# Seven block products for nine tenths of the last gate and up projections, with weight sums made by adding DMAs and VectorE

## The chip, the cores and the metric

The kernel runs on one NeuronCore of a Trainium2 chip. The metric is the time of one execution on the device in microseconds (us): the median of several runs. The core has TensorE (PE in the rows, with its weight loads as PEld), VectorE (DVE), ScalarE (ACT), GpSimd (POOL) and SyncE (SP), which issues most transfers. They run side by side and wait for one another through semaphores.

## The reference, cut to what matters

Two transformer blocks run one after the other over 16 + 512 tokens of width 1024. The stage in question is the last one but one of the second block, the gate and up projections of its feed-forward part:

```python
def swiglu(hn, w_ffn_in, w_ffn_out):
    a, b = jnp.split(hn @ w_ffn_in, 2, axis=-1)
    return (jax.nn.silu(a) * b) @ w_ffn_out

        ff = swiglu(rmsnorm(h, norm_ffn_pre[l]), w_ffn_in[l], w_ffn_out[l])
        h = h + rmsnorm(ff, norm_ffn_post[l])
    return h[:, N_META:]
```

`w_ffn_in` has 1024 rows and 2 x 2816 columns, `w_ffn_out` 2816 rows. Only the last 512 tokens are returned, so in this last part only they are computed.

## The kernel before

Everything is held transposed: feature rows on the 128 partitions, tokens along a partition. `h` is eight such tiles (KT = 8, the 1024 features), and a product of 128 output features takes eight weight tiles of 128 x 128 as stationary operand and the 512 tokens as moving operand.

**Splitting.** The products must be accurate to nearly float32, and TensorE's fast form (`float32r`) rounds its operands. So each operand is a rounded part and a rest: weights `wh` and `wl`, activations `xh` and `xl`. A product is three matmuls, `wh*xh + wh*xl + wl*xh` (L460 for 512 tokens in one PSUM bank, L464 for two halves of 264). One load of 128 output features is a *unit*: 8 tiles, 512 KB. SP fetches it into one of four slots of `raw` (L408), ScalarE rounds it into `wh` (L423), VectorE subtracts to get `wl` (L427), and TensorE runs its 24 matmuls. `wh` and `wl` have two slots each, so unit u+2 may be rounded only when TensorE has finished unit u. ScalarE and VectorE each see one such operation of 1024 columns per unit.

**The last up stage** is `PH_UP2`: 11 rounds of the loop, each with two hidden tiles of 128, each of these a gate unit and an up unit. That is 22 pairs of units (FT = 22), 44 units, 1056 matmuls of 512 columns. For each pair VectorE multiplies both PSUM results with `rstd` (L1872, the factor of the norm), ScalarE applies Silu (L1303), VectorE multiplies (L1920), ScalarE rounds the hidden tile into `hidh` (L1234) and VectorE subtracts for `hidl` (L1927).

**The stage behind it**, `PH_DOWN2`, makes eight output tiles of 22 hidden tiles each, in three units of 8, 7 and 7. Its first group asks for the hidden tiles one after the other by the semaphore `hid_ready`; then VectorE copies the result out of PSUM (L2563).

**Order of the work.** Each engine runs a program written out by hand, strictly in order. `split_ahead` puts the rounding (ScalarE) and the rest (VectorE) of the next unit between the operations on finished products. PE waits for `w_split` (the rest is there) and for `psum_free` (the bank is empty). GpSimd does nothing between the sum of squares at the start of the stage (`pool_ssq(pool, 5, META)`) and the next such sum.

```python
        for n, (w, x) in enumerate(((wh, hi), (wh, lo), (wl, hi))):
            last = nc.tensor.matmul(ps[:, bank, 0:SEQ], w[:, slot, kk, :],
                                    x[:, k0 + k, x.shape[2] - SEQ:x.shape[2]], start=first, stop=end_)
```

## Time and profile before

| | |
|---|---|
| Time, median of 3 runs | 2833.64 us (2832.86 to 2834.41) |
| Profiled execution, first to last instruction (span) | 2830.8 us |
| What lies around the span (median less span) | 2.8 us |
| TensorE matmul busy | 2769.5 us, 98% of the span |
| VectorE, ScalarE, GpSimd busy | 1599.3, 1197.5 and 186.2 us |
| Unbroken run of 1050 matmuls, most of the last up stage and the first down group | 2462.01 to 2705.23 us |
| The last part, 2706 us to the end | 125 us |

The profiled execution has no time of its own beside its span; the table gives the span and the median of the runs. Matmuls overlap in their pipeline, so a matmul's own duration (about 395 ns) says little: what counts is the time from one to the next, which is read from the chain of waits or from the timeline.

### The profile page before, as it was taken

The numbers are of one execution on the slowest core, as the hardware profiler recorded it, in microseconds if no ns is written. First come the engines' busy times: TensorE is split into PE (matmuls) and PEld (weight loads), VectorE is DVE, ScalarE is ACT, GpSimd is POOL, SyncE is SP. The second block draws the span as 40 slices with busy tenths as digits, with TensorE's granted clock in tenths as the row PEclk, the third lists the DMA queues.
The fourth block names the chain that finished last, engine by engine and source line by source line (L and its number), as shares of the span: only waits on it lengthen the run. The fifth ranks groups of instructions, "written<-read, shape, count | busy, mean of one in ns | idle before, by whom it ended". The sixth has DMA issues, their size and how long they took to land.

```text
span 2830.8 us, 46604 instructions
## 1 busy us (share of the span) xinstructions
PE 2769.5 (98%) x17661; PEld 2474.3 (87%) x17661; DVE 1599.3 (56%) x2385; ACT 1197.5 (42%) x1933; POOL 186.2 (7%) x160
## 2 busy tenths in 40 slices
PE   7999999999989999999999999999999999899998
PEld 7899899999989999899988888887899988688886
DVE  6777745554367776655543453553577775644422
ACT  4445543332245554433332223232478883422232
POOL 2000010000021221000000010010100000000000
PEclk9999999999999999999999999999999999999999
DMA  4222123333331111233323322323222223233322
GB/s 124 67 75 67 53 83 89 89 89 90 89 102 53 52 52 45 76 96 89 95 87 100 93 75 77 94 65 92 84 59 59 59 60 90 75 96 96 91 86 76
DMA packets 417672, 225.65 MB, mean 80 GB/s; under 512 B 7493, under 2 KB 414278, under 8 KB 417462
## 3 DMA queue, kind: packets, MB, share of 16 engines
q1 hardware_dynamic: 414550, 211.45, 25.7%
q0 software_dynamic: 2256, 10.32, 1.2%
q10 hardware_dynamic: 784, 2.75, 0.3%
q8 instruction: 56, 0.92, 0.1%
q14 instruction: 26, 0.21, 0.0%
HBM read 222.36 MB, written 2.13 MB: 79 GB/s over the span
## 4 chain that ended last, share of the span: by engine, by line
PE 62%; DVE 5%; issue 2%; ACT 2%; POOL 0%; DVEq 0%; ACTq 0%; POOLq 0%
PE ps L460 34%; PE ps L464 17%; PE ps L906 2%; PE ps L1064 2%; PE ps L1105 1%; PE ps L1094 1%; PE ps L1126 1%; DVE wl L427 1%; PE ps L1031 1%; PE ps L951 1%; PE ps L1017 0%; DVE rl L2363 0%; PE ps L1098 0%; PE ps L940 0%; PE ps L1052 0%
## 5 line engine op out<-in xcount | busy, mean ns | idle before, releaser
L423 ACT ACTIVATE wh<-raw 128x1024 fp32r<-128x1024 f32 (+3 forms) x423 | 425.1, 1007 | 739.5 <-PE ps L460 390.4
L427 DVE TENSOR_TENSOR wl<-raw,wh 128x1024 fp32r<-128x1024 f32 (+3 forms) x423 | 506.9, 1198 | 329.7 <-ACT wh L423 326.5
L464 PE MATMUL ps<-xh,wh 128*128 128x264 f32 x2736 | 569.6, 289 | 9.9 <-DVE xl L494 5.9
L464 PE MATMUL ps<-xl,wh 128*128 128x264 f32 x2736 | 558.7, 286 | 0.0
L464 PE MATMUL ps<-xh,wl 128*128 128x264 f32 x2736 | 558.2, 285 | 0.0
L464 PEld LDWEIGHTS ps<-xh,wh 128*128 128x128 f32 x2736 | 428.7, 189 | 19.7 <-issue 8.9
L464 PEld LDWEIGHTS ps<-xl,wh 128*128 128x128 f32 x2736 | 426.0, 189 | 0.0
L464 PEld LDWEIGHTS ps<-xh,wl 128*128 128x128 f32 x2736 | 425.2, 189 | 0.0
L460 PE MATMUL ps<-xh,wh 128*128 128x512 f32 x960 | 382.5, 398 | 3.5 <-DVE wl L427 3.4
L460 PE MATMUL ps<-xl,wh 128*128 128x512 f32 x960 | 379.6, 395 | 0.0
L460 PE MATMUL ps<-xh,wl 128*128 128x512 f32 x960 | 377.6, 393 | 0.0
L460 PEld LDWEIGHTS ps<-xh,wh 128*128 128x128 f32 x960 | 180.3, 188 | 47.7 <-issue 6.1
L460 PEld LDWEIGHTS ps<-xh,wl 128*128 128x128 f32 x960 | 180.6, 188 | 40.7
L460 PEld LDWEIGHTS ps<-xl,wh 128*128 128x128 f32 x960 | 180.1, 188 | 41.0 <-issue 1.4
L460 PE MATMUL ps<-hidh,wh 128*128 128x512 f32 x352 | 138.8, 394 | 0.4 <-DVE wl L427 0.4
L460 PE MATMUL ps<-hidh,wl 128*128 128x512 f32 x352 | 138.9, 395 | 0.0
L460 PE MATMUL ps<-hidl,wh 128*128 128x512 f32 x352 | 138.1, 392 | 0.0
L1872 DVE TENSOR_TENSOR pre<-ps,rstd 128x528 f32<-128x528 f32 (+1 forms) x66 | 46.4, 702 | 161.7 <-PE ps L464 110.4
L1872 DVE TENSOR_TENSOR t<-ps,rstd 128x512 f32<-128x512 f32 (+1 forms) x66 | 46.0, 697 | 141.9 <-PE ps L460 100.0
L1872 DVE TENSOR_TENSOR rt<-ps,rstd 128x512 f32<-128x512 f32 (+1 forms) x53 | 36.9, 697 | 140.2 <-PE ps L460 100.8
L507 POOL COPY ssq<-sq 128x528 f32<-128x528 f32 (+1 forms) x6 | 4.6, 763 | 1356.4 <-ACT sq L490 1075.6
L1787 POOL TENSOR_TENSOR g_d<-post_t 128x528 f32<-128x528 f32 (+1 forms) x56 | 68.6, 1243 | 246.4 <-ACT g_e L1440 158.3
(380 smaller groups left out, 4205.8 us busy)
## 6 DMA issues: line engine op xcount, KB each, us to landing
raw<-in_w_in SPq DMA_DIRECT2D x88, 512.0 KB, 3.9
raw<-in_ffn_w_gate SPq DMA_DIRECT2D x44, 512.0 KB, 3.7
raw<-in_ffn_w_up SPq DMA_DIRECT2D x44, 512.0 KB, 3.7
raw<-in_w_ffn_in SPq DMA_DIRECT2D x44, 512.0 KB, 3.7
raw<-in_fox_w_in SPq DMA_DIRECT2D x33, 512.0 KB, 4.1
raw<-in_hgrn_w_in SPq DMA_DIRECT2D x32, 512.0 KB, 3.9
raw<-in_ffn_w_down SPq DMA_DIRECT2D x32, 448.0 KB, 3.5
raw<-in_ffn_w_down SPq DMA_DIRECT2D x16, 512.0 KB, 3.9
```

The costliest lines, as they stand in the source:

```text
L423: nc.scalar.activation(wh[:, v % 2, 0:nk, :], raw[:, v % RAW_SLOTS, 0:nk, :], ACT.Copy).then_inc(s("w_hi"), 1)
L427: nc.vector.tensor_tensor(wl[:, v % 2, 0:nk, :], raw[:, v % RAW_SLOTS, 0:nk, :], wh[:, v % 2, 0:nk, :].bitcast(F32), ALU.subtract).then_in ...
L460: last = nc.tensor.matmul(ps[:, bank, 0:SEQ], w[:, slot, kk, :], x[:, k0 + k, x.shape[2] - SEQ:x.shape[2]], start=first, stop=end_)
L464: last = nc.tensor.matmul(ps[:, bank + b, 0:HALF], w[:, slot, kk, :], x[:, k0 + k, b * HALF:(b + 1) * HALF], start=first, stop=end_)
L906: last = nc.tensor.matmul(ps[:, 2 + k % 2, P * c:P * (c + 1)], left[:, P * c:P * (c + 1)], right[:, P * c:P * (c + 1)], start=True, stop=True)
L951: last = nc.tensor.matmul(flat[:, at:at + TOK[j]], g_left[:, j * (j - 1) // 2 + c, :], g_f[:, P * j:P * j + TOK[j]], start=True, stop=True)
L1031: last = nc.tensor.matmul(flat[0:TOK[j], at:at + SEQ - QFIRST[j]], rt[:, 2 + c, P * j:P * j + TOK[j]], rt[:, c, META + QFIRST[j]:L], start ...
L1064: last = nc.tensor.matmul(ps[:, 4 + e, QFIRST[j]:SEQ], r_vt[0:k, j, P * e:P * (e + 1)], r_s[0:k, QSTRIP[j]:QSTRIP[j] + SEQ - QFIRST[j]], s ...
L1094: nc.tensor.matmul(flat[:, QSTRIP[j]:QSTRIP[j] + SEQ - QFIRST[j]], s_kp[:, b, P * j:P * j + P], q[:, QFIRST[j]:SEQ], start=(j < 3 and n == ...
L1105: return nc.tensor.matmul(dst, w[:, :], src, start=False, stop=last, skip_group_check=True)
L1787: nc.gpsimd.tensor_tensor(hgrn_halves(g_d[:, hgrn_buffer(n), 0:cols_], n), b, b[:, :, width - 1:width].to_broadcast([P, cols_ // (2 * widt ...
L1872: return V.tensor_tensor(shown(ph, gj, dst), out_of(ph, gj), shown(ph, gj, rstd[:, :]), ALU.mult)\
```

## The change

Rounds 0 and 1 of the last up stage (4 pairs) stay. The other 18 pairs, phase `PH_DUO2`, are computed differently. A pair is seen as a 2 x 2 matrix of blocks, (gate, up) by (input features of k = 0..3, k = 4..7), that multiplies a 2 x 2 matrix (the same halves of k) by (tokens 0..255, tokens 256..511). Strassen's scheme in Winograd's form gives the four results of two rows and two columns with seven block products in place of eight. One block product is 4 weight tiles x 3 matmuls = 12 matmuls of 256 columns, so a pair takes 84 matmuls of 256 columns in place of 48 of 512.

- **Right-hand sums.** The sums and differences of activation blocks (`xb`, `xc`, `xa`, `xd`, each of 4 x 256 columns) are built once, by VectorE and ScalarE between the operations of rounds 0 and 1 (`x_sums`, `x_rests`), and split into rounded part and rest.
- **Left-hand sums**, per pair: four sums of weight blocks. GpSimd issues three DMAs per pair (`add_up`): gate's first half into `w_sum1`, up's second half *added* onto up's first half in `raw`, up's first half *added* onto `w_sum1`. VectorE makes the other two (`w_sum`), in `w_sum2`.
- **Splits**, per pair: seven of 512 columns on ScalarE (`duo_hi`) and on VectorE (`duo_lo`), where there were two of 1024.
- **Results**, per pair: two products are accumulated in PSUM on top of earlier ones, two others likewise; ScalarE copies two blocks of 256 out and VectorE combines five of 256. Only the gate is multiplied with `rstd`; the factor of the up half is moved behind the down stage, where the copy becomes a multiplication (L2951 in the changed kernel).
- **Hidden tiles** are kept in float32 (`hid2`) and split only at the end: the area of `hidh` is used by the sums until then. All 22 roundings (`hid_hi`) and rests (`hid_lo`) stand in the last pair and in the first group of the down stage.
- Semaphores of other stages are merged (`dve_step`, `pool_step`, `r_rot_step`), with the same waits.

```diff
-PH_UP2 = Phase(PH_OUT, FT // 2, K8, [(1, 3, 2 * (_g % 2), 2 - 2 * (_g % 2))[(b - _g) % 4] for b in range(4)], narrow=range(4))
-PH_DOWN2 = Phase(PH_UP2, 2, [list(DOWN_K)] * 4, narrow=range(4))
+PH_UP2 = Phase(PH_OUT, 2, K8, [(1, 3, 2 * (_g % 2), 2 - 2 * (_g % 2))[(b - _g) % 4] for b in range(4)], narrow=range(4))
+PH_DUO2 = Phase(PH_UP2, FT // 2 - PH_UP2.n, K8)
+PH_DOWN2 = Phase(PH_DUO2, 2, [list(DOWN_K)] * 4, narrow=range(4))
+DUO_SLOT, DUO_BANK = (0, 1, 2, 3, 0, 1, 2), (4, 5, 6, 7, 4, 6, 7)
+DUO_FREE = (-2, -1, 0, -3, 1, 2, 3)
...
+        return (first_[:, 0:4, :], w_sum2[:, :, :], second[:, 0:4, :], w_sum1[:, :, :], first_[:, 4:8, :], w_sum2[:, :, :],
+                second[:, 4:8, :])[p]
...
+            for uj in range(4):
+                slot, count = duo_unit(i, uj // 2, uj % 2)
+                if first(i):
+                    sp.wait_ge(s("w_split"), unit(PH_DUO2, 0, uj) + 1)
+                else:
+                    sp.wait_ge(s("p_split"), 7 * (2 * i + uj // 2 - 1))
+                sp.dma_start(raw[:, slot, :, :], (fu if uj % 2 else fg)(i, P * (uj // 2))).then_inc(s(f"w_loaded{slot}"), 16)
...
+            for p in range(7):
+                if begin and p == 0:
+                    pe.wait_ge(s("rstd_ready"), 7)
+                elif begin and p == 1:
+                    pe.wait_ge(s("x_ready"), KT * 6 + 23)
+                elif p == 0 and not begin:
+                    pe.wait_ge(s("p_copied"), 2 * g)
+                elif p < 4 and not begin:
+                    pe.wait_ge(s("p_out"), 6 * g + (-5, -2, 0)[p - 1])
...
+                pe.wait_ge(s("p_split"), duo_split(i, mm, p))
+                hi, lo = x_parts[p][0:2]
+                for k in range(KT // 2):
+                    for n, (w, x) in enumerate(((wh, hi), (wh, lo), (wl, hi))):
+                        last = nc.tensor.matmul(ps[:, DUO_BANK[p], 0:DUO_W], duo_slot(w, p)[:, k, :], x[:, k, :],
+                                                start=(p < 4 and k + n == 0), stop=(k == KT // 2 - 1 and n == 2),
+                                                skip_group_check=True)
...
+        def add_up(i, mm):
...
+            if not begin:
+                pool.wait_ge(s("p_split"), 4 if first(i) else duo_split(i, mm, 3) - 7)
+            pool.dma_start(w_sum1[:, :, :], g2(i, P * mm)[:, 0:4, :]).then_inc(s("pool_loaded0"), 16)
+            pool.wait_ge(s(f"w_loaded{slot}"), 16 * count)
+            pool.dma_start(raw[:, slot, 0:4, :], u2(i, P * mm)[:, 4:8, :], accum_op=ALU.add).then_inc(s("pool_loaded1"), 16)
+            pool.wait_ge(s("pool_loaded0"), bank0 + 32 * g + 16)
+            pool.dma_start(w_sum1[:, :, :], u2(i, P * mm)[:, 0:4, :], accum_op=ALU.add).then_inc(s("pool_loaded0"), 16)
...
+            V.tensor_tensor(w_sum2[:, :, :], w_sum2[:, :, :] if n else w_sum1[:, :, :],
+                            duo_source(i, mm, 4 if n else 6), ALU.add).then_inc(s("p_sums"), 1)
...
+            if last:
+                for k in range(10):
+                    hid_hi(k)
...
-                V.tensor_copy(ff[:, 4 * i + mm, :], out_of(PH_DOWN2, mm)).then_inc(s("psum_free"), 1)
+                V.tensor_tensor(ff[:, 4 * i + mm, :], out_of(PH_DOWN2, mm), rstd[:, META:L], ALU.mult).then_inc(s("psum_free"), 1)
```

VectorE, one pair in the middle of the stage. Before (the second half of a round: `pre` and `t_124` are the scaled gate and up, `t_123` the hidden tile, `wl` the rests of the weights):

```order
L1872 TENSOR_TENSOR pre_122<-ps,rstd 128x512 [waits mm_done,rstd_ready]
L427 TENSOR_TENSOR wl<-raw,wh 128x1024 [waits w_hi]
L1872 TENSOR_TENSOR t_124<-ps,rstd 128x512 [waits mm_done]
L1920 TENSOR_TENSOR t_123<-t_123,t_124 128x512 [waits silu,psum_free]
L427 TENSOR_TENSOR wl<-raw,wh 128x1024 [waits w_hi]
L1927 TENSOR_TENSOR hidl_121<-t_123,hidh_120 128x512 [waits hid_hi]
```

Now, from the hidden tile of the pair before to the split that opens the pair behind (`w_sum_138` is `w_sum1`, `w_sum_139` is `w_sum2`, `sq` holds blocks copied out of PSUM):

```order
L2856 TENSOR_TENSOR hid_128<-t_123,t_124 128x512 [waits silu,p_out]
L2874 TENSOR_TENSOR sq<-sq,ps 128x256 [waits p_mm,p_copied]
L2837 TENSOR_TENSOR wl<-w_sum_139,wh 128x512 [waits p_hi]
L2878 TENSOR_TENSOR sq<-ps,sq 128x256 [waits p_out,p_mm]
L2837 TENSOR_TENSOR wl<-raw,wh 128x512 [waits p_hi]
L2885 TENSOR_TENSOR t_124<-ps,sq 128x256 [waits p_out,p_mm]
L2832 TENSOR_TENSOR w_sum_139<-w_sum_138,raw 128x512 [waits pool_loaded0,w_loaded2,w_loaded1]
L2837 TENSOR_TENSOR wl<-w_sum_138,wh 128x512 [waits p_hi]
L2837 TENSOR_TENSOR wl<-raw,wh 128x512 [waits p_hi]
L2897 TENSOR_TENSOR pre_122<-ps,sq 128x256 [waits p_mm]
L2900 TENSOR_TENSOR pre_122<-pre_122,rstd 128x512 [waits p_copied,p_out]
L2837 TENSOR_TENSOR wl<-w_sum_139,wh 128x512 [waits p_hi]
```

Six operations became sixteen (the four ahead of these twelve are `wl`, `t_124`, `w_sum_139`, `wl`), and the sum in the middle waits for GpSimd's last DMA.

ScalarE, the last pair and the start of the down stage in the changed kernel:

```order
L1327 ACTIVATE wh<-raw 128x512 [waits w_loaded2,p_mm]
L1327 ACTIVATE hidh_120<-hid_128 128x512 [waits psum_free] x3
L1327 ACTIVATE hidh_120<-hid_128 128x512 [waits p_mm,psum_free]
L1327 ACTIVATE hidh_120<-hid_128 128x512 [waits p_mm,hid] x6
L1327 ACTIVATE pre_122<-ps 128x256 [waits p_mm]
L1327 ACTIVATE wh<-raw 128x512 [waits w_loaded3]
L1327 ACTIVATE wh<-raw 128x512 [waits p_mm]
L1838 ACTIVATE t_123<-pre_122 128x512 [waits p_out]
L1327 ACTIVATE hidh_120<-hid_128 128x512 [waits p_mm,hid] x4
L448 ACTIVATE wh<-raw 128x896 [waits p_mm,mm_done,w_loaded0]
```

Before, one rounding of a hidden tile stood between two units; now ten stand ahead of the first rounding of down weights.

## Rows read from the trace of the kernel before

**Rows 1.** The page: busy time and share of each engine; granted clock in tenths.
```profile
PE 2769.5 (98%) x17661; PEld 2474.3 (87%) x17661; DVE 1599.3 (56%) x2385; ACT 1197.5 (42%) x1933; POOL 186.2 (7%) x160
PEclk9999999999999999999999999999999999999999
```

**Rows 2.** Chain of waits in order of time: start us, us, what.
```profile
1711.44 11.76 PE ps L464 x96
...
2462.01 243.22 PE ps L460 x1050
```

**Rows 3.** Windows: stretch, us, busy PE, PEld, DVE, ACT, POOL, clock, DMA share, GB/s.
```profile
2431.00:2438.00 7.00, 1.10 (x2) 0.28 (x2) 4.59 (x6) 5.25 (x7) 0.00 (x0) 0.89 0.26 77
2438.00:2446.00 8.00, 7.02 (x15) 4.64 (x16) 7.86 (x13) 4.76 (x9) 0.00 (x0) 0.50 0.00 0
...
2452.00:2456.00 4.00, 3.51 (x16) 2.59 (x15) 2.59 (x4) 2.09 (x2) 0.00 (x0) 1.00 0.00 0
2462.00:2706.00 244.00, 244.00 (x1060) 197.94 (x1059) 112.10 (x133) 75.36 (x93) 0.00 (x0) 1.00 0.32 95
```

**Rows 4.** Timeline, PE: matmuls of other widths, each start counts.
```profile
2054.73 0.29 PE L1094 MATMUL ps<-s_qh,s_kp 128*128 128x272 f32 x1
2054.85 0.29 PE L1094 MATMUL ps<-s_ql,s_kp 128*128 128x272 f32 x1
2054.97 0.23 PE L1094 MATMUL ps<-s_qh,s_kp 128*128 128x144 f32 x1
...
2322.36 0.70 PE L1098 MATMUL ps<-later_r,ident_r 128*128 128x112 f32 x5
2322.92 0.91 PE L1126 MATMUL ps<-s_sh,s_vp 128*128 128x512 f32 x5
```

**Rows 5.** Timeline, DVE: operations of 512 and 272 columns close together.
```profile
1929.71 0.67 DVE L427 TENSOR_TENSOR wl<-raw,wh 128x512 fp32r<-128x512 f32 x1
1930.31 0.67 DVE L2377 TENSOR_TENSOR yr<-yr,ps 128x512 f32<-128x512 f32 x1
1930.91 0.68 DVE L427 TENSOR_TENSOR wl<-raw,wh 128x512 fp32r<-128x512 f32 x1
...
2312.56 0.45 DVE L2456 TENSOR_TENSOR s_e<-s_e 128x272 f32<-128x272 f32 x1
2312.92 0.68 DVE L2450 TENSOR_TENSOR s_sl<-s_e,s_sh 128x512 fp32r<-128x512 f32 x1
...
2455.13 3.87 DVE L2550 TENSOR_TENSOR ssq<-ssq,yr 128x512 f32<-128x512 f32 x5
```

**Rows 6.** Timeline around the end of a unit: what follows the last matmul.
```profile
2606.43 0.40 PE L460 MATMUL ps<-xh,wh 128*128 128x512 f32 x1
...
2606.63 1.06 ACT L423 ACTIVATE wh<-raw 128x1024 fp32r<-128x1024 f32 x1 [3.20 <-PE ps L460]
2606.63 0.69 DVE L1872 TENSOR_TENSOR pre<-ps,rstd 128x512 f32<-128x512 f32 x1 [2.32 <-PE ps L460]
```

**Rows 7.** Groups of instructions, shapes apart: ScalarE's rounding, VectorE's rest, GpSimd's DMA issue.
```profile
L423 ACT ACTIVATE wh<-raw 128x512 fp32r<-128x512 f32 x32 | 20.2, 632 | 91.0 <-PE ps L460 69.7 <-PE ps L464 21.2
L427 DVE TENSOR_TENSOR wl<-raw,wh 128x1024 fp32r<-128x1024 f32 x42 | 51.3, 1222 | 10.3 <-ACT wh L423 10.3
L1772 POOL DMA_DIRECT2D crep<-c_scratch x16 | 8.6, 540 | 260.3 <-DVE t_rows L2021 258.0 <-DMA c_scratch<-fx 2.2
```

**Rows 8.** DMA issues of the page: count, KB each, us from issue to landing.
```profile
raw<-in_w_ffn_in SPq DMA_DIRECT2D x44, 512.0 KB, 3.7
crep<-c_scratch POOLq DMA_DIRECT2D x16, 264.0 KB, 3.5
rotary<-in_t_rotary POOLq DMA_DIRECT2D x1, 528.0 KB, 3.9
restart<-in_t_restart POOLq DMA_DIRECT2D x1, 264.0 KB, 3.1
```

**Rows 9.** Chain of waits: four ScalarE copies in a row, late in the kernel.
```profile
2788.76 1.95 ACT f_tok L1234 x4
```

More of the change, by code:

```diff
@@ L1740, in _, with duo_body @@
+        def duo_body(i):
+            for mm in range(2):
+                duo(i, mm)
+        duo_hi(0, 0, 0)
+        duo_hi(0, 0, 1)
+        duo_body(0)
+        loop(act, PH_DUO2.n - 1, duo_body, 1)
+        duo(PH_DUO2.n - 1, 0)
+        duo(PH_DUO2.n - 1, 1, True)
         for m in range(KT):
@@ L1743, in _ @@
                 split_ahead(act, act_hi, PH_DOWN2, i, 3 * mm + n, i == 1)
+                if m == 0 and n < 2:
+                    for k in range(14 + 4 * n, 18 + 4 * n):
+                        hid_hi(k)
             if m < 4:
@@ new lines, in w_sum @@
+        def w_sum(i, mm, n):
+            g = 2 * i + mm
+            if n == 0:
+                for m in range(2):
+                    slot, count = duo_unit(i, mm, m)
+                    dve.wait_ge(s(f"w_loaded{slot}"), 16 * count)
+                dve.wait_ge(s("pool_loaded0"), 16 * (FOX_H // 2) + 32 * g + 32)
+            V.tensor_tensor(w_sum2[:, :, :], w_sum2[:, :, :] if n else w_sum1[:, :, :],
+                            duo_source(i, mm, 4 if n else 6), ALU.add).then_inc(s("p_sums"), 1)
@@ new lines, in _, with duo_body @@
+        gate2(0, 0)
+        hid2_classic(0, 0)
+        gate2(0, 1)
+        hid2_classic(0, 1)
+        split_ahead(dve, dve_lo, PH_UP2, 1, 0)
+        x_sums(0)
+        gate2(1, 0)
+        split_ahead(dve, dve_lo, PH_UP2, 1, 1)
+        x_sums(2)
+        hid2_classic(1, 0)
+        split_ahead(dve, dve_lo, PH_UP2, 1, 2)
+        gate2(1, 1)
+        x_rests(0)
+        w_sum(0, 0, 0)
+        duo_lo(0, 0, 0)
+        duo_lo(0, 0, 1)
+        hid2_classic(1, 1)
+        x_rests(1)
+        def duo_body(i):
+            for mm in range(2):
+                duo(i, mm)
```

334 lines of the change are left out of this document (300 added, 34 removed).

## The prediction

> **What bounds the kernel now.** The page comes first: TensorE is busy for 98% of the span, and its granted clock is at nine tenths or more in every slice [rows 1]. A busy matmul row is not yet a matmul at its peak, so the second view is the chain of waits. There the last up stage is one unbroken run of TensorE, 1050 matmuls of 512 columns in 243.22 us, 231.6 ns each [rows 2]. In the windows of that stage the clock is 1.00, that is 2.4 GHz, VectorE is busy for 112.1 us of 244, ScalarE for 75.4, GpSimd for nothing, and the 16 DMA engines for 0.32 at 95 GB/s [rows 3]. So TensorE sets this stage alone, VectorE has half its time free, and less work for TensorE is time saved, as long as nobody makes it wait.
>
> **What the seven products take away.** Before, 18 pairs x 48 matmuls x 231.6 ns = 200.1 us. Now, 18 x 84 matmuls of 256 columns. No row has 256 columns. Those of 264 come every 122.5 ns (11.76 us for 96, [rows 2]), those of 272 every 0.12 us [rows 4]. From 264 to 512 a column costs (231.6 - 122.5) / 248 = 0.44 ns, so eight fewer leave 119.0 ns. From above the bound is 122.5 (nothing gained on 264), from below 112 ns, the spacing of five matmuls of 112 columns ((2322.92 - 2322.36) / 5, [rows 4]), where the columns no longer count. I take 119.0, since 264 is by far the nearest. A block product is then 1.43 us, a pair 10.0 us, where it was 11.1, and the stage 179.9 us: **20.2 us less** (14.9 to 30.8 by the bounds). For the matmul spacing the Trainium skill ("TensorE: Matmul & The Clock Gate", Back-to-back issue gap) gives N / 2.4 + 2.5 ns. For 512 columns that is 215.8, and the trace has 231.6, so the measurement decides; by the page 256 columns would take 109.2 ns, the stage 165.1 us, and the saving would be 35.0 us.
>
> **VectorE in a pair.** Nine operations of 512 columns on SBUF (seven rests, two sums). Independent ones start 0.60 us apart [rows 5]: 5.4. Five of 256 columns: those of 272 take 0.36 to the next start, so 0.35: 1.75. The scaling of the gate and the hidden tile each need the result just before, and such a row is 0.77 (3.87 us for 5): 1.55. Together 8.7 us of 10.0. Before it was two of 1.22 and four of 0.69, 5.2 us of 11.1 [rows 6, 7]. It fits, with 1.3 us to spare. ScalarE has seven roundings of 0.63 at most [rows 7], one Silu and two copies, 5.8 us.
>
> **GpSimd's transfers** are new, and the sums that VectorE makes wait for them. Their issue is 0.54 us each [rows 7], beside nothing. A plain GpSimd transfer of 264 KB lands after 3.1 and 3.5 us [rows 8]; I take 3.3. An adding transfer is in no row. From below it is a plain one, 3.1 (nothing excludes that the adding is free). From above it is two landings one after the other, 7.0. It reads its target too, so the nearest row is the one of twice the bytes, rotary, 528 KB in 3.9 us: I take 3.9. With it there are two loops:
> - *The area of `w_sum1`*: rest of product 3, plain transfer 3.3, adding transfer 3.9, sum 0.7, rest 0.7 (0.60 and 0.1 for the semaphore): 8.6 us, under 10.0. TensorE is held up once the adding transfer takes over 5.3.
> - *The slots of `raw`*: SP's two loads of 512 KB start when the rest of product 6 is made, about 6 us into a pair. One lands in 3.7 [rows 8]; the second behind it 1.8 later, by 95 / 0.32 = 297 GB/s while the engines are busy. GpSimd's two issues take 0.6 more for the second, and 3.9: 10.0 us behind the start, 6 us into the next pair, just when VectorE gets there (6 to 6.5). TensorE needs the block that hangs on it at 10.0, with two rests ahead: some 2 us of slack, about 1 after VectorE's own order.
>
> So I cost the steady stage at nothing beyond TensorE's 10.0. The cover is thin: without it, each microsecond per pair costs 18.
>
> **Start of the stage.** Building the sums (16 + 5 operations of VectorE, most of 256 columns) lies in rounds 0 and 1, 44 us in which VectorE is half idle: nothing. But the last two rests of the sums, each 1.2 us [rows 7], stand behind the last hidden tile of round 1. That begins 0.2 us after TensorE goes on [rows 6]: 0.2 + 0.6 + 2.4 = 3.2 us, and product 1 wants them at 1.4. **1.8 us.** In the second pair GpSimd's first transfer waits for the fourth rest, 3.2 + 2 x 0.6 + 0.1 = 4.5; 3.3 + 3.9 give 11.7; sum and two rests 13.7; TensorE is there at 11.8. With 0.3 for the rest behind it: **2.2 us.** Later pairs have the lead of a whole pair and pay nothing.
>
> **End of the stage.** In the last pair ScalarE has its last rounding of weights done at about 5.5 us; then come ten roundings of hidden tiles ahead of the copy of the gate and of the first down weights. Copies in a row take 0.49 (1.95 for 4, [rows 9]), roundings 0.63 at most; 0.55 each gives 11.0, the copy 11.3, the first half of the weights 11.95. VectorE then has that half's rest, the gate's sum, its scaling and the other half's rest, 2.1 us: 14.0. TensorE has been free since 10.0. **4.0 us.** The second down unit's rest stands behind eight more rests of hidden tiles, the last hidden tile and its own rounding; counted the same way TensorE waits another **1.5 us**. From the third unit on it is ahead. Before, each hidden tile was split on the way and this seam cost nothing.
>
> **Clock.** After the idle 7 us at 2431 the clock was 0.50 for the next 8 us, that is 1.2 GHz; after 2.5 us of idle time at 2453 it stayed 1.00 [rows 3]. The 4.0 us at the end lie between: 0 from below, 4 from above (8 us at half the rate). I take **1.0**. Merged semaphores and `rstd` in the place of a copy (0.69 either way) cost nothing: same waits, same sizes.
>
> **Sum**: -20.2 + 1.8 + 2.2 + 5.5 + 1.0 = -9.7 us. Against the profiled span of 2830.8 that is 2821.1. The median of the runs lies 2.8 above the span, and so does the forecast: 2833.64 - 9.7 = 2824 us, 0.34% faster. A measurement of this kernel tells about 0.2%, 5.7 us, from no change.
>
> **Rivals.**
> - *A. The adding transfers share the DMA engines and become the bound, narrowly.* A pair moves 1 MB by SP, 0.25 plain and 0.5 MB adding, and if both sources are read that is 2.25 MB, 7.9 us of 10.0 at 297 GB/s. Then an adding transfer lands in 4.8, and 0.9 is lost in the crowd: 3.3 + 0.9 + 4.8 + 1.4 = 10.4 us a pair. +0.4 x 18 and +1 in the second pair: -1.5, 2832 us. For it: three transfers are issued within a microsecond of each other. Against: 0.32 of the engines is all that is used now. The Trainium skill ("Collectives: The Full Stack", Part 3, on the bandwidth ceiling) says that an add in the DMA engine costs no cycles of its own but two source reads, and measured half the rate; no row here shows it. Chance 0.17.
> - *B. Slower: the adding transfer is a long one.* Reading the target, adding and writing back are done chunk by chunk, with 512 B pieces, and it lands after 6 to 7 us. VectorE stands at the first sum of every pair and all its later rests with it; TensorE stalls at product 0. Each us over 5.3 costs 18 and one more in the second pair. It is slower than before from 5.8 us; at 7.0 a pair takes 11.7, and the time is -9.7 + 1.7 x 19 = +22.6, 2856 us. For it: nothing in the trace bounds it better. Against: twice the bytes land 0.4 to 0.8 later in plain form. Chance 0.20.
> - *C. VectorE becomes the bound.* Sixteen operations with up to three waits each in place of six; if each loses 0.1 us on waits and on the loop's address arithmetic, it has 10.3 to 10.4 a pair. +7, 2831 us. For it: 8.7 of 10.0 has no slack for bad luck, and it waits for products as well. Against: 0.60 from start to start in rows with waits. Chance 0.12.
> - *D. 256 columns go no faster than 264*, since a weight load belongs to every matmul: +5.3, 2829 us. The 0.12 for 272 speaks for a shallow slope. Chance 0.06.
> - *E. 256 columns go as fast as the narrow ones*, 112 ns [rows 4]: -10.6 more, 2813 us. Against: 264 columns are far from it, and each width read so far pays for its columns. Chance 0.02. The page's 109.2 ns would be this case.
> - That the change does not do what it says can hardly be: the order of the instructions has 84 matmuls of 256 columns per pair.
>
> **Numbers.** The forecast has 0.43; A 0.17, B 0.20, C 0.12, D 0.06, E 0.02. Faster by over 0.2%: 0.43 + 0.03 (A) + 0.04 (C) + 0.02 (E) = 0.52. Within 0.2%: 0.09 + 0.05 + 0.06 = 0.20. Slower: 0.20 (B) + 0.05 + 0.03 = 0.28. The likeliest case alone gives 2819 to 2828. The range reaches down to 2818 (end of the stage at half its price, no clock lost, a little under 119 ns) and up to 2850, which takes in A, C, D and B up to an adding transfer of 6.7 us; about 0.1 is left out on each side.
>
> **What would show it.** Right: chain pieces of TensorE of about 10.0 us per pair without a gap, matmuls 119 ns apart, VectorE at 85 to 90% in the stage, adding transfers landing in about 4 us, gaps of about 2, 2, 4 and 1.5 us at the four places. Wrong: TensorE idle ahead of product 0 of every pair, with VectorE's sum released by a DMA (A or B, by the landing time), or VectorE without idle time and TensorE waiting for its rests (C); a clock below 1.00 in the stage; a spacing of 122 ns or more (D).

## The result, and the profile after

| | before | after | ratio (95% interval) |
|---|---|---|---|
| Median of 4 runs each | 2834.02 us | 2860.8 us (2859.22 to 2861.59) | 1.0097 (1.0084 to 1.011) |
| Span of the profiled execution | 2830.8 us | 2859.4 us | |

The change makes the kernel 27 us slower. The forecast was 9.7 us faster, and 2860.8 lies outside its range.

The page of the kernel after, busy time by engine and the parts of its queue table and DMA issues that belong to the change:
```profile
PE 2764.0 (97%) x18309; PEld 2498.9 (87%) x18309; DVE 1687.4 (59%) x2603; ACT 1248.9 (44%) x2071; POOL 246.7 (9%) x214
q0 software_dynamic: 22704, 24.48, 4.5%
raw<-in_w_ffn_in SPq DMA_DIRECT2D x44, 512.0 KB, 5.7
w_sum<-in_w_ffn_in POOLq DMA_DIRECT2D x36, 256.0 KB, 4.4
```
Against [rows 1], TensorE is busy for 5.5 us less in a span that is 28.6 us longer: it waits. Against [rows 8], SP's loads of `w_ffn_in` land 2 us later (5.7 for 3.7).

The windows of the kernel after, columns as in [rows 3]: the first pair and the start of the second, from there into the ninth, the pairs up to the last, and the end of the stage.
```profile
2492.00:2516.00 24.00, 13.38 (x98) 13.03 (x99) 14.08 (x23) 7.35 (x15) 5.46 (x5) 0.87 0.43 89
2516.00:2602.00 86.00, 78.01 (x613) 76.79 (x613) 64.18 (x117) 38.78 (x73) 24.26 (x22) 0.94 0.74 150
2602.00:2705.00 103.00, 91.86 (x745) 88.31 (x744) 76.82 (x142) 46.39 (x89) 27.34 (x25) 1.00 0.74 150
2705.00:2716.00 11.00, 7.51 (x64) 7.33 (x63) 9.69 (x19) 8.62 (x17) 0.00 (x0) 0.93 0.53 152
```
Before, TensorE had no idle time in this stage. Now it is idle for about a tenth of every long window, and VectorE is idle too (76.82 of 103): neither of them is the bound. The DMA share has gone from 0.32 to 0.74.

The timeline of TensorE after, only the matmuls that start behind idle time (what stands in brackets), in the first two pairs, and two later ones:
```profile
2493.33 0.36 PE L1281 MATMUL ps<-xh,wh 128*128 128x256 f32 x1 [1.74 <-DVE wl L2837]
...
2496.71 0.38 PE L1281 MATMUL ps<-xbh,wh 128*128 128x256 f32 x1 [1.72 <-DVE xdl L2821]
...
2513.00 0.55 PE L1281 MATMUL ps<-xh,wh 128*128 128x256 f32 x1 [7.57 <-DVE wl L2837]
...
2666.63 0.39 PE L1281 MATMUL ps<-xh,wh 128*128 128x256 f32 x1 [0.97 <-DVE wl L2837]
...
2677.73 0.39 PE L1281 MATMUL ps<-xh,wh 128*128 128x256 f32 x1 [0.59 <-DVE wl L2837]
```
Twelve matmuls of a product take 1.415 us wherever TensorE isn't held up, 117.9 ns each, so a pair could take 9.91. The starts of product 1 of the fifth and the 18th pair are 2551.88 and 2703.62: 11.67 us a pair. The second pair begins with a wait of 7.6 us for VectorE's rest of product 0. The third, fifth and seventh have none there, the fourth and sixth 3.2 and 2.8 us. From the eighth on every pair has one, of 0.6 to 1.5 us and 2.6 in the last. VectorE in its turn waits for a transfer:

Waits for the transfers in the kernel after, 2510 to 2740 us (engine line, what it waited for: us in total, times, longest):
```profile
ACT wh L1327 <- DMA w_sum<-in_w_ffn_in: 67.4, 16, 10.2
DVE w_sum L2832 <- DMA w_sum<-in_w_ffn_in: 47.7, 16, 9.1
...
POOL raw L2036 <- DMA raw<-in_w_ffn_in: 29.8, 14, 4.3
PE ps L1281 <- DVE wl L2837: 25.8, 14, 7.6
```

**Where the time went**, by the starts of the products. The stage (2491.56 to 2715.84) takes 224.3 us for 200.1: the 18 pairs at 9.91 would be 178.5, 21.6 less. Against that stand 1.8 us ahead of product 0 and 2.0 ahead of product 1 of the first pair, 9.1 more for the second pair, 29.3 for the 16 after it (1.8 each), and 3.5 behind the last. The first down group takes 17.95 us for 15.28, and the stage begins 1.7 us later than in the execution before. This last seems no part of the change: the traces of e3 and e4 below, where nothing is different for TensorE up to there, begin it 1.4 us earlier. 24.2 + 2.7 + 1.7 = 28.6, the difference of the spans.

### The profile page after: what moved, and what is told of

It reads as the page before. It is cut to its first block, busy times and chain, and to the rows that moved or that the text cites. A ratio compares the mean times of both kernels' runs of the same rounds, so it can differ in the third digit from the quotient of the medians.

```text
span 2859.4 us, 48876 instructions
## 1 busy us (share of the span) xinstructions
PE 2764.0 (97%) x18309; PEld 2498.9 (87%) x18309; DVE 1687.4 (59%) x2603; ACT 1248.9 (44%) x2071; POOL 246.7 (9%) x214
## 4 chain that ended last, share of the span: by engine, by line
PE 50%; DVE 5%; DMA 4%; issue 3%; ACT 2%; POOL 0%; SPq 0%; DVEq 0%; POOLq 0%; ACTq 0%
PE ps L485 27%; PE ps L489 14%; DMA w_sum<-in_w_ffn_in 2%; DMA raw<-in_w_ffn_in 2%; PE ps L1122 2%; PE ps L1163 1%; PE ps L1281 1%; PE ps L1152 1%; PE ps L1184 1%; PE ps L964 1%; PE ps L1089 1%; DVE wl L2837 1%; DVE wl L452 1%; PE ps L1075 0%; DVE rl L2579 0%
## 5 line engine op out<-in xcount | busy, mean ns | idle before, releaser
L448 ACT ACTIVATE wh<-raw 128x1024 fp32r<-128x1024 f32 (+3 forms) x386 | 386.0, 1002 | 608.2 <-PE ps L489 335.1
L452 DVE TENSOR_TENSOR wl<-raw,wh 128x1024 fp32r<-128x1024 f32 (+3 forms) x386 | 462.0, 1197 | 317.6 <-ACT wh L448 314.4
L489 PEld LDWEIGHTS ps<-xh,wh 128*128 128x128 f32 x2736 | 428.1, 189 | 19.4 <-issue 8.7
L489 PEld LDWEIGHTS ps<-xl,wh 128*128 128x128 f32 x2736 | 425.5, 189 | 0.0
L489 PEld LDWEIGHTS ps<-xh,wl 128*128 128x128 f32 x2736 | 424.5, 189 | 0.0
L485 PE MATMUL ps<-xh,wh 128*128 128x512 f32 x672 | 270.2, 402 | 3.5 <-DVE wl L452 3.5
L485 PE MATMUL ps<-xl,wh 128*128 128x512 f32 x672 | 266.2, 396 | 0.0
L485 PE MATMUL ps<-xh,wl 128*128 128x512 f32 x672 | 264.8, 394 | 0.0
L485 PEld LDWEIGHTS ps<-xh,wh 128*128 128x128 f32 x672 | 126.5, 188 | 34.8 <-issue 6.1
L485 PEld LDWEIGHTS ps<-xh,wl 128*128 128x128 f32 x672 | 126.7, 189 | 28.7
L485 PEld LDWEIGHTS ps<-xl,wh 128*128 128x128 f32 x672 | 126.5, 188 | 28.5 <-issue 1.4
L530 POOL TENSOR_TENSOR ssq<-ssq,sq 128x528 f32<-128x528 f32 (+1 forms) x41 | 59.4, 1448 | 356.6 <-ACT sq L515 252.0
L1281 PE MATMUL ps<-xh,wh 128*128 128x256 f32 x216 | 63.4, 293 | 27.6 <-DVE wl L2837 27.6
```

Source lines behind the costliest of these rows:

```text
L448: nc.scalar.activation(wh[:, v % 2, 0:nk, :], raw[:, v % RAW_SLOTS, 0:nk, :], ACT.Copy).then_inc(s("w_hi"), 1)
L452: nc.vector.tensor_tensor(wl[:, v % 2, 0:nk, :], raw[:, v % RAW_SLOTS, 0:nk, :], wh[:, v % 2, 0:nk, :].bitcast(F32), ALU.subtract).then_in ...
L489: last = nc.tensor.matmul(ps[:, bank + b, 0:HALF], w[:, slot, kk, :], x[:, k0 + k, b * HALF:(b + 1) * HALF], start=first, stop=end_)
L530: nc.gpsimd.tensor_tensor(ssq[:, t0:L], ssq[:, t0:L], sq[:, m % 2, t0:L], ALU.add).then_inc(s("sq_used"), 1)
L1281: last = nc.tensor.matmul(ps[:, DUO_BANK[p], 0:DUO_W], duo_slot(w, p)[:, k, :], x[:, k, :], start=(p < 4 and k + n == 0), stop=(k == KT // ...
```

## The experiments

Theory of the forecast, with its price corrected: the adding transfers land too late (**length**). Rivals: they use up the DMA engines and everything lands late (**sharing**); VectorE is the bound; and, formed after e5 and e8, GpSimd's transfer into `w_sum1` stands in its queue behind a wait that doesn't concern it (**queue**). The pairs' time is the mean from the fifth to the 18th pair in the trace; in the change it is 11.67. The traces are of single executions, which for e8 took 8.4 us more than the median and for e9 8.4 us less. In e2, e3, e14, e15 and e16 sums are left out, so their results are not the reference's.

| Run | What is different | us | ratio to before (95%) | us a pair |
|---|---|---|---|---|
| e3_no_sums | no weight sums, no GpSimd transfers | 2820.6 | 0.9957 (0.9938 to 0.9977) | 9.91 |
| e2_plain | both adding transfers plain | 2832.1 | 0.9995 (0.9984 to 1.0007) | 9.97 |
| e14_raw_plain | only the one into `raw` plain | 2847.4 | 1.0044 (1.0028 to 1.0059) | 11.10 |
| e15_w1_plain | only the one into `w_sum1` plain | 2845.5 | 1.004 (1.0024 to 1.0055) | 10.89 |
| e1_w1_first | order of the two turned round | 2867.4 | 1.0118 (1.0088 to 1.0147) | 12.60 |
| e6_raw_dve | `raw` sum on VectorE | 2850.1 | 1.0056 (1.0039 to 1.0073) | 11.17 |
| e5_double | two buffers for `w_sum1` | 2858.4 | 1.0084 (1.0067 to 1.01) | 12.10 |
| e11_double_first | and its transfer first | 2833.0 | 0.9995 (0.9986 to 1.0005) | 10.78 |
| e16_first_plain | and the one into `raw` plain | 2820.7 | 0.9961 (0.9946 to 0.9976) | 9.91 |
| e4_two_w1 | two buffers, `raw` sum on VectorE | 2820.3 | 0.9954 (0.9931 to 0.9977) | 9.91 |
| e8_spare | e4 and an unused adding transfer, behind the wait for the load | 2856.8 | 1.0075 (1.0058 to 1.0091) | 12.11 |
| e9_spare_plain | the same, plain | 2859.1 | 1.0093 (1.0077 to 1.0108) | 11.74 |
| e10_spare_last | adding, but last and without that wait | 2820.9 | 0.9959 (0.9943 to 0.9974) | 9.91 |
| e7_all_dve | all four sums on VectorE | 2824.1 | 0.9965 (0.9953 to 0.9978) | 10.10 |
| e12_seams | e4 with both ends of the stage mended | 2815.7 | 0.9938 (0.9924 to 0.9952) | 9.91 |
| e13_seams2 | and the second down unit's split earlier | 2814.7 | 0.9939 (0.9925 to 0.9952) | 9.91 |

**What the sums cost in all, and how much of it is the adding.** e3_no_sums takes the weight sums out altogether, e2_plain lets the two transfers write instead of add:
```diff
-            pool.dma_start(raw[:, slot, 0:4, :], u2(i, P * mm)[:, 4:8, :], accum_op=ALU.add)...
+            pool.dma_start(raw[:, slot, 0:4, :], u2(i, P * mm)[:, 4:8, :])...
...
-            pool.dma_start(w_sum1[:, :, :], u2(i, P * mm)[:, 0:4, :], accum_op=ALU.add)...
+            pool.dma_start(w_sum1[:, :, :], u2(i, P * mm)[:, 0:4, :])...
```


> Edit: no weight sums at all; GpSimd's three transfers and VectorE's two sums are left out, the splits read raw instead, so the results are not the reference's. TensorE's work is that of the changed kernel. It is the floor of the scheme. My sum (20.2 saved, 4.0 + 1.5 at the end, 1.8 at the start) gives 2834.0 - 20.2 + 7.3 + 1 = 2822; with the 1.8 more that product 0 of the first pair waited for ScalarE, 2824. If VectorE or ScalarE bound the stage (V), gaps ahead of product 0 of every pair stay and it is over 2835.

> Edit: the two adding transfers of a pair become plain ones of the same size at the same places, so the weight sums are left out of them and the results are not the reference's. Theory L: a plain transfer lands in 3.4 where the adding one took 4.7 to 5.4, and its issue takes 0.78 where it took 1.27; the chain shortens by about 3 us, below TensorE's 9.9, and only the seams are left: about 18 x 1.4 = 25 us less than the changed kernel, 2835. Rival B: the bytes read fall from 2.25 to 1.75 MB a pair, so if the engines are full it gains as well, but then SP's loads must still take about 6 us. Rival V: no change, 2860.

Measured: 2820.6 and 2832.1. Without sums the saving of the seven products is there, seams included: 40 us of the change's time are the sums. With plain transfers the later pairs are within 0.06 us of TensorE's, and 28.7 of the 40 us are gone; of the other 11.5 most, 9.3, lies in the second to the fourth pair. So transfers hold the pairs, and the adding decides. Which chain of them it is, this pair of runs doesn't tell.

**One adding transfer at a time** (e14 and e15, half of that diff each):

> The change (2860.8) with the transfer into raw writing instead of adding (its sum is then wrong); w_sum1 keeps its adding transfer and its single buffer, behind it in GpSimd's queue. If the w_sum1 loop alone holds the pairs, they stay at about 11.3 us, as in e6_raw_dve where GpSimd had no transfer into raw at all (2850): 2848 to 2856. If the length of the adding transfer into raw holds them, 2832 to 2840.

> The change with the second transfer into w_sum1 writing instead of adding (its sum is wrong); the one into raw still adds. The w_sum1 loop gets some 2 us shorter (3.4 for 5.4), but still stands in the queue behind the wait for SP's load and an adding issue of 1.3 us. If the two loops hold the pairs together, 2838 to 2850; if w_sum1's length alone does, 2830 to 2834 as with both plain; if the transfer into raw does, no change, 2855 or more.

Measured: 13.4 and 15.3 us less than the change, together just the 28.7 of both. e14 is half a microsecond under what was expected if the loop of `w_sum1` alone holds the pairs. Why each of the two brings about half is read from the loop itself, below.

**The order of the two.** e1 swaps the last two transfers of `add_up`:

> Edit: GpSimd issues the adding transfer into w_sum1 ahead of the one into raw. Theory L (latency: the chain from the rest of product 6 over SP's two loads, GpSimd's add into raw and its add into w_sum1 holds every pair): w_sum1's add no longer stands behind the loads, only the loop of w_sum1 itself is left, 0.7 + 3.4 + 5.4 + 1.4 = 10.9 us a pair in place of 11.4, so about 9 us less than the changed kernel, 2851. Rival B (the DMA engines are full): the same bytes move, no change, 2860. Rival V (VectorE is the bound): no change either, 2860.

Wrong: 2867.4, nothing gained. It is 6.6 us over the change, though from two runs and with intervals that overlap. The chain of waits, one pair of it (start us, us, what), has no load of SP and no transfer into `raw` in it, only the two transfers into `w_sum1`:
```profile
2621.48 5.65 DMA w_sum<-in_w_ffn_in
...
2627.74 5.13 DMA w_sum<-in_w_ffn_in
2632.89 0.64 ACT wh L1327
2633.56 0.70 DVE wl L2837
...
2634.93 3.93 DMA w_sum<-in_w_ffn_in
```
The queue no longer stands in their way, and the pairs are not faster. The plain transfer now often runs beside the adding one into `raw` and lands after 4.7 us in the mean, where it took 3.5 in the change. ScalarE waits for `w_sum1` for 53.8 us, 13 times, and for `raw` for 18.7, ten times.

**One cause taken out at a time.** e6 leaves GpSimd nothing but `w_sum1`:
```diff
-            pool.wait_ge(s(f"w_loaded{slot}"), 16 * count)
-            pool.dma_start(raw[:, slot, 0:4, :], u2(i, P * mm)[:, 4:8, :], accum_op=ALU.add)...
...
+            if n == 0:
+                up0 = duo_source(i, mm, 2)
+                V.tensor_tensor(up0, up0, duo_source(i, mm, 6), ALU.add).then_inc(s("p_sums"), 1)
```


> The change with the sum into raw taken from GpSimd and given to VectorE (one more VectorE sum a pair, 1.22 us), w_sum1 still a single buffer with one plain and one adding transfer. VectorE then has 8.7 + 1.2 = 9.9 us a pair. Theory S (the single w_sum1 binds at 11.7 us a pair, less what GpSimd no longer queues ahead of its adding issue): 10.4 to 11.2 us a pair, 2832 to 2846. Theory R (the adding transfer into raw, behind the load, is what binds): with it gone the pairs are at TensorE's 9.9, 2820 to 2826. A landing of the w_sum1 transfer near 4.4 instead of 5.4 would show that its length came from meeting the other.

Measured: 2850.1. The single buffer alone is enough to hold the pairs, at 11.17 us. The chain of waits of e6, one pair of it (start us, us, what), shows the loop bare:
```profile
2600.49 0.70 DVE wl L2836
...
2601.94 3.21 DMA w_sum<-in_w_ffn_in
...
2605.28 0.79 issue
...
2606.09 4.41 DMA w_sum<-in_w_ffn_in
...
2610.53 0.06 DVE w_sum L2828
...
2611.74 0.70 DVE wl L2836
```
From one rest of product 3 to the next 11.25 us: the rest 0.70, 0.75 until GpSimd begins to issue the plain transfer, 3.21 from there to its landing, then 0.93 until it begins to issue the adding one, 4.41, and 1.21 for two sums (0.6 of which the change has on GpSimd). The forecast had 8.6 for this loop; the two delays ahead of an issue, 1.7 us, weren't in it.

**The loop that holds the change.** The same loop can be laid out in every run with one buffer for `w_sum1`, from the starts of GpSimd's issues and their landings. The means from the fifth to the 18th pair, in us:

| Run | first transfer lands | to the second issue | second lands | to the next pair's first issue | sum | TensorE's pair |
|---|---|---|---|---|---|---|
| the change | 3.48 | 0.65 | 5.32 | 2.16 | 11.61 | 11.67 |
| e14_raw_plain | 3.51 | 0.67 | 4.85 | 2.10 | 11.13 | 11.10 |
| e15_w1_plain | 3.51 | 0.67 | 4.63 | 2.16 | 10.97 | 10.89 |
| e2_plain | 3.58 | 0.69 | 3.59 | 2.08 | 9.93 | 9.97 |
| e1_w1_first | 4.69 | 0.69 | 5.06 | 2.10 | 12.54 | 12.60 |
| e6_raw_dve | 3.38 | 0.71 | 4.50 | 2.62 | 11.20 | 11.17 |

What stands between the landings hardly changes: 2.1 us are ScalarE's rounding, VectorE's rest and the delay ahead of the issue, with VectorE's `raw` sum 2.6. What differs is how long the transfers take, and the pairs follow. e14 shortens the second landing although it changes the other transfer; in e15 the second transfer is plain, but is issued right behind an adding one, and takes 4.6 us where it took 3.6 in e2. So each of the two brings about half.

The change has GpSimd's wait for SP's load in this loop too, and yet it costs nothing there. GpSimd's rows of the change (L2034 the plain transfer into `w_sum1`, L2036 the one into `raw`, L2038 the adding one into `w_sum1`), and the landings of the first and the last of the three over 2600 to 2650 us:
```profile
2608.14 0.78 POOL L2034 DMA_DIRECT2D w_sum<-in_w_ffn_in  x1 [5.70 <-DVE wl L2837]
2611.38 1.27 POOL L2036 DMA_DIRECT2D raw<-in_w_ffn_in  x1 [2.45 <-issue]
2612.22 1.73 POOL L2038 DMA_DIRECT2D w_sum<-in_w_ffn_in  x1
2619.92 0.78 POOL L2034 DMA_DIRECT2D w_sum<-in_w_ffn_in  x1 [5.97 <-DVE wl L2837]
2622.57 1.29 POOL L2036 DMA_DIRECT2D raw<-in_w_ffn_in  x1 [1.86 <-DMA raw<-in_w_ffn_in]
2624.17 1.29 POOL L2038 DMA_DIRECT2D w_sum<-in_w_ffn_in  x1 [0.31 <-issue]
2631.40 0.78 POOL L2034 DMA_DIRECT2D w_sum<-in_w_ffn_in  x1 [5.95 <-DVE wl L2837]
```
```profile
DMA to landing us min/median/max: 3.4/3.4/3.5
```
```profile
DMA to landing us min/median/max: 4.9/5.6/5.9
```
In all 17 pairs of the stage that have these three transfers GpSimd was past the wait for SP's load before the plain transfer had landed (2622.57 against 2619.92 + 3.4). The adding one was issued 0.62 us behind that landing in most, 0.87 at the latest. So the single buffer holds the change. Its chain of waits leads over SP's load all the same, because GpSimd's issue into `raw` ends behind that landing, here at 2623.86.

e5 gives `w_sum1` a second buffer and leaves the rest:
```diff
-            if not begin:
-                pool.wait_ge(s("p_split"), 4 if first(i) else duo_split(i, mm, 3) - 7)
-            pool.dma_start(w_sum1[:, :, :], ...
+            if not first(i):
+                pool.wait_ge(s("p_split"), 7 * g - 10)
+            pool.dma_start(w_sum1[mm][:, :, :], ...
```


> The change with one thing more: two buffers for w_sum1, used in turn, so that GpSimd starts the plain transfer of the next pair a pair early; the sum into raw is still GpSimd's adding transfer. Theory S (the two loops are short each by itself, and the single w_sum1 is the shorter one: 0.7 + 3.4 + 0.8 + 5.4 + 1.4 = 11.7 us a pair against the 9.9 of TensorE): the pairs fall to the raw loop, about 10.0 to 10.5 us, and the kernel to 2825 to 2836. Theory R (the loop over the slots of raw binds: load 6.6, issue 2.2, adding landing 5.2 where the forecast had 5.5 + 0.6 + 3.9): nothing changes but some tenths, 2852 to 2862. Theory I (two adding transfers in flight together lengthen each other, as in the run with the order of the two turned round): they now meet more often, and it is slower, 2862 or above.

Measured: 2858.4, theory R's range. The second pair no longer loses 9 us, but the later ones take 12.1. Its GpSimd rows show why (start us, us, what, and in brackets the idle time before):
```profile
2616.13 1.29 POOL L2036 DMA_DIRECT2D raw<-in_w_ffn_in  x1 [8.30 <-DMA raw<-in_w_ffn_in]
2616.95 1.78 POOL L2038 DMA_DIRECT2D w_sum1b<-in_w_ffn_in  x1
2617.89 1.63 POOL L2034 DMA_DIRECT2D w_sum<-in_w_ffn_in  x1
```
GpSimd stands for 8 us ahead of the transfer into `raw`, until SP's load has landed. The transfer into `w_sum1` needs nothing of that load, its area has long been ready, and it is issued only now. Then three transfers run together. With the loop of the single buffer gone the queue holds the pairs, and by chance about as long.

e4 has both edits, the second buffer and the `raw` sum on VectorE:

> Edit: two buffers for w_sum1, so that GpSimd makes it a pair earlier; the sum in raw is made by VectorE (three sums there, one adding transfer on GpSimd). Results as the reference's. Theory L: no transfer is on the path of a pair any more; VectorE has 9.3 us of work in 9.9, so the pairs run at 9.9 to 10.2 and the time is 2824 to 2830, faster than the kernel before. Rival B: 0.5 MB less is read a pair; loads still slow, about 2850. Rival V: VectorE has more work, and it is slower than the changed kernel or equal to it, 2860 to 2870.

Measured: 2820.3, better than the range: no pair waits, with VectorE busy for 94.98 of 100 us. From e6 it differs by the second buffer alone, which is worth 29.8 us here.

**Sharing or queue?** e4 leaves room to load the engines on purpose. e8 adds to it one adding transfer of 256 KB a pair into an area nobody reads, behind the wait for SP's load; e9 makes it plain; e10 puts it last, without the wait:
```diff
+            pool.wait_ge(s(f"w_loaded{slot}"), 16 * count)
+            pool.wait_ge(s("masks_loaded"), 16 + 16 * (2 * i + mm))
+            pool.dma_start(w_spare[:, :, :], u2(i, P * mm)[:, 4:8, :], accum_op=ALU.add)...
             pool.wait_ge(s(f"pool_loaded{mm}"), bank0 + 32 * i + 16)
             pool.dma_start(w_sum1[mm][:, :, :], u2(i, P * mm)[:, 0:4, :], accum_op=ALU.add)...
```


> The version with two w_sum1 buffers and three sums on VectorE (2820.3) and, beside it, one more adding transfer of 256 KB a pair of the same rows of up, into a spare buffer that nobody reads or waits for but GpSimd's next transfer into it: the traffic and the queue of the change without its waits. Theory S or R (what costs is that TensorE's weights wait for the end of the adding transfer): 2820 to 2823. Theory of sharing (adding transfers take the loads' room on the DMA engines and delay SP's loads and the other adding transfer): the loads' landing goes from 4.2 towards 5.7 us, the w_sum1 transfer from 5.3 towards 7, and the kernel is over 2830.

> As e8_spare (2856.8), but the spare transfer writes instead of adding: the same bytes read and the same place in GpSimd's queue, behind the wait for SP's load of up. In the traces an adding transfer takes 33.7 us of DMA engine for its 256 KB, a plain one 14.9. Theory of the queue (the w_sum1 transfer is issued late because GpSimd stands in front of the spare one until SP's load has landed, 8 to 9 us a pair): still 2850 or more. Theory of the adding transfer's weight: near 2820 to 2828.

> As e8_spare, but the spare adding transfer stands last in GpSimd's queue, behind the w_sum1 one, and doesn't wait for SP's load: the traffic alone. Theory of the queue: 2820 to 2826. Theory of sharing (the adding transfers load the DMA engines to about nine tenths of a 9.9 us pair: 2 x 30.2 + 14.9 + 2 x 33.7 = 142.7 us of 16 engines = 8.9 us, and SP's loads come late): 2835 to 2857.

Measured: 2856.8, 2859.1 and 2820.9. e8 alone would have spoken for sharing, and would have misled: the same traffic in another place of the queue (e10) costs nothing, and a much lighter transfer in the same place (e9) costs about the same. GpSimd's waits, 2550 to 2680 us, first of e9, then of e10:
```profile
POOL w_spare L2041 <- DMA raw<-in_w_ffn_in: 79.8, 9, 9.8
```
```profile
POOL w_sum1b L2033 <- DMA w_sum1b<-in_w_ffn_in: 20.4, 6, 3.6
POOL w_sum L2033 <- DMA w_sum<-in_w_ffn_in: 16.7, 5, 3.6
```
In e10 the adding transfer of `w_sum1` waits only for its own plain one. Its window says how full the engines may be without harm (columns as in [rows 3]):
```profile
2520.00:2600.00 80.00, 80.00 (x681) 80.00 (x680) 75.93 (x137) 43.96 (x80) 26.92 (x24) 1.00 0.88 184
```
DMA share 0.88, TensorE without a gap. Sharing as a bound by itself falls. It lengthens landings: in e10 the adding transfer into `w_sum1` takes 6.9 us (median), which two buffers hide.

**The change's own work, in a better order.** e11 is e5 with the transfer into `w_sum1` ahead of the wait for SP's load:
```diff
-            pool.wait_ge(s(f"w_loaded{slot}"), 16 * count)
-            pool.dma_start(raw[:, slot, 0:4, :], u2(i, P * mm)[:, 4:8, :], accum_op=ALU.add)...
             pool.wait_ge(s(f"pool_loaded{mm}"), bank0 + 32 * i + 16)
             pool.dma_start(w_sum1[mm][:, :, :], u2(i, P * mm)[:, 0:4, :], accum_op=ALU.add)...
+            pool.wait_ge(s(f"w_loaded{slot}"), 16 * count)
+            pool.dma_start(raw[:, slot, 0:4, :], u2(i, P * mm)[:, 4:8, :], accum_op=ALU.add)...
```


> As e5_double (2858.4: two w_sum1 buffers, both sums by adding transfers), but the w_sum1 transfer is issued ahead of GpSimd's wait for SP's load, the one into raw behind it. All of the change's work by the same engines. Theory of the queue: 2822 to 2832, the pairs at TensorE's 9.9 to 10.3 us. Theory of sharing: 2845 or more, since both adding transfers are still there; then the loads of SP land at 5.5 us or later.

> e11_double_first (2833.0: two buffers, w_sum1's adding transfer ahead of the wait for SP's load) with the transfer into raw writing instead of adding. If the 12 us that e11 keeps over 2821 are the raw loop (load 7.2, then adding landing 6.1), they go: 2820 to 2824. If they are the two-buffer loop of w_sum1 or VectorE, they stay: 2830 or more.

Measured: 2833.0, just above the range of the queue theory and 25.4 us under e5; with a plain transfer into `raw` (e16) 2820.7. The DMA issues of e11, 2550 to 2650 us:
```profile
raw<-in_w_ffn_in SPq DMA_DIRECT2D x20, 512.0 KB, 7.2
w_sum<-in_w_ffn_in POOLq DMA_DIRECT2D x10, 256.0 KB, 5.8
raw<-in_w_ffn_in POOLq DMA_DIRECT2D x10, 256.0 KB, 6.1
```
So the order was worth 25 us, and what is left, 12 us, is the loop over the slots of `raw`: a load of 7.2 us and an adding transfer of 6.1 behind it, both stretched by running beside each other; in e16, where they take 5.1 and 3.4, the 12 us are gone. Here sharing does its part, through the length of a chain.

**All sums on VectorE** (e7: GpSimd's transfers taken out, `w_sum1` and the `raw` sum made by two more operations of 512 columns):

> All four weight sums on VectorE, no transfer of GpSimd in the stage. VectorE has 8.7 + 2 x 1.22 = 11.1 us a pair, and no wait for a transfer other than SP's loads. If VectorE is as busy as the sum of its instructions says, the pairs are 11.1 to 11.5 us, 1.2 to 1.6 above TensorE's 9.9, and with 17 of them the kernel takes 2820 + 20 to 27 = 2840 to 2847: slower than before, quicker than the change. If what cost the change its gain is the weights' path and VectorE can hide more than that, it is below 2835.

Measured: 2824.1, pairs of 10.10 us. The expectation was wrong by its price: 1.22 us is VectorE's time for 1024 columns [rows 7]; these sums have 512, 0.60 each, so VectorE has 9.9 us a pair. It is now the bound, by 0.2 us a pair (window 2550 to 2650 us):
```profile
2550.00:2650.00 100.00, 100.00 (x833) 98.41 (x832) 97.50 (x179) 54.86 (x100) 0.00 (x0) 1.00 0.38 105
```

**The ends of the stage**, on top of e4. e12, cut to its core:
```diff
+                if i and mm:
+                    act.wait_ge(s("x_ready"), KT * 6 + 16)
+                    copy(xb[0][:, :, :], xb[2][:, :, :]).then_inc(s("xh_ready"), 1)
...
                 silu2(mm)
...
-                for k in range(10):
+                for k in range(6):
                     hid_hi(k)
...
-        gate2(1, 1)
         x_rests(0)
-        w_sum(0, 0, 0)
+        gate2(1, 1)
+        x_rests(1)
         duo_lo(0, 0, 0)
+        w_sum(0, 0, 0)
```


> On e4_two_w1 (2820.3), the two ends of the stage alone. Start: ScalarE rounds the x sums ahead of the last silu of the ordinary rounds, where it idled 5.2 us, and VectorE takes the rests there too, so products 0 and 1 of the first pair shouldn't wait (1.7 and 1.7 us now). End: four of the ten roundings of hidden tiles and VectorE's bank 5 work stand behind the split of down's first weights, so the stall of 3.5 us there shrinks to about 0.5 to 1, and with it the stretch at half clock behind it (9 matmuls at 0.43 instead of 0.23 us, 1.8). Together 6 to 8 us: 2812 to 2815. If the seams were hidden by something else, 2818 to 2821.

> e12_seams (2815.65) with the split of down's second unit of weights (0.93 of ScalarE, 1.08 of VectorE) ahead of four more roundings of hidden tiles and their rests. In e12's trace TensorE still waits 1.29 us at down's first unit and 2.10 at its second, the latter for this rest. The second goes: 2813 to 2814. If the hidden tiles' rests then come late instead, 2815 to 2817.

Measured: 2815.7 and 2814.7. The two waits at the start are gone, 3.9 us in the traces. At the end e4 had the first row, e12 the next two:
```profile
2676.08 0.77 PE L486 MATMUL ps<-hidh,wh 128*128 128x512 f32 x1 [3.48 <-issue]
```
```profile
2669.05 0.47 PE L486 MATMUL ps<-hidh,wh 128*128 128x512 f32 x1 [1.29 <-issue]
...
2676.94 0.50 PE L486 MATMUL ps<-hidh,wh 128*128 128x512 f32 x1 [2.10 <-DVE wl L453]
```
2.2 us are saved ahead of the first down unit, but nothing in all: the first down group took 17.0 us in e4, with 1.7 of half clock behind the wait, and takes 19.4 in e12, since 2.1 are lost ahead of the second unit and the half clock now comes behind that. So the start alone brought most of the 4.7 us, where 6 to 8 were expected of both. In e13's trace the 2.10 has gone and 0.67 stands ahead of the third unit; its runs can't be told from e12's. These two are the fastest versions found, e13 0.61% under before (0.48 to 0.75), some 1.6% under the change.

## Why the prediction was wrong

- **Matmul spacing 119.0 ns**: right, 117.9. The saving of 20.2 us is 21.6. D and E fall.
- **VectorE in a pair, 8.7 us of 10.0**: right. It takes three sums with 0.60 each in e4 and still isn't the bound. C falls for the change; two more sums (e7) bring it about.
- **"*The area of `w_sum1`* ... 8.6 us, under 10.0"**: the step that failed. This loop takes 11.6 us in the change (table above): plain transfer 3.5, delay ahead of the next issue 0.65, adding transfer 5.3, and 2.15 for rounding, rest and the delay ahead of the next issue. Of the 3.0 us too little, 1.4 are the adding transfer, 0.2 the plain one and 1.4 the two delays.
- **"An adding transfer is in no row ... I take 3.9"**: it landed in 4.5 us (e6, median), in the change in 4.7 into `raw` and 5.3 into `w_sum1`, in the second pair in 8.8. The bounds of 3.1 and 7.0 held it in the steady stage, but the row taken as nearest, a plain transfer of twice the bytes, isn't like it.
- **"Their issue is 0.54 us each ..., beside nothing"**: a plain issue is 0.78 and an adding one 1.27 us, up to 1.8 behind another. This is inside the time to landing, but the 0.65 and some 0.7 us between the end of a wait and the start of the issue are not, and they lie on the loop. With them it has room for an adding transfer of 9.9 - 3.5 - 0.65 - 2.15 = 3.6 us, not the 5.3 of the forecast. A plain one just fits (e2), an adding one didn't in any run.
- **"With it there are two loops"**: right for the change, where the first alone holds the pairs. What it leaves out is GpSimd's queue, which joins them once `w_sum1` has two buffers. That is worth 25 us there (e5 to e11), and nothing in the change.
- **"So I cost the steady stage at nothing beyond TensorE's 10.0. The cover is thin"**: 1.8 us a pair, 29.3 us. The sentence behind it, that each microsecond a pair costs 18, was right.
- **Start**: 1.8 at product 1, measured 2.0. Not foreseen: 1.8 at product 0, because ScalarE rounds all x sums ahead of the first weights. **Second pair**: 2.2, measured 9.1. Its first transfer is issued 4.8 us after product 0, where the forecast had 4.5; the adding one then meets two of SP's loads and takes 8.84, and TensorE begins again at half clock.
- **End**: 4.0 and 1.5 with 1.0 for the clock; measured 3.5, nothing, and 2.7 for the clock: eleven matmuls at 0.43 us behind the wait, and no wait at the second unit. The sum is right (6.5 and 6.2) by luck.
- **Rivals**: B was the nearest, and its result came (2856 forecast, 2860.8). Its mechanism, the adding transfer too long for the loop, is the right one, but the number is luck: at the measured 5.3 us B costs nothing by the forecast's limit of 5.3, and it comes true only with the two delays that no rival had. A, sharing, had the DMA share about right, but as a bound it falls by e10; it lengthens the landings. The Trainium skill ("Collectives: The Full Stack", Part 3, on the bandwidth ceiling) says an add costs two source reads and measured half the rate. The traces fit that: 14.9 us of one DMA engine for 256 KB plain (27.9% of 16 engines in 100 us, 30 transfers, e2), 33.7 adding (30.4% for ten of each, e4), 2.3 times. But the adding transfers also go in smaller pieces (below), and no run tells the two apart. Here it sets the length, not a ceiling.

A wait in an in-order queue shows only when the buffer behind it is free: the other order brought nothing with one buffer (e1) and 25.4 us with two (e5 to e11).
